# First-block slabs in halves and in place, evictions ahead of weight quarters, a reordered gate stage, and values computed inside the differential heads

## The reference

```python
# first block
mod = silu(c) @ w_ada + b_ada                      # c (1, 1024), w_ada (1024, 6144)
sh1, sc1, g1, sh2, sc2, g2 = split(mod, 6)
mix = token_mixer(x * (1 + sc1) + sh1)             # 8 attention heads of 64 over 64 keys chosen
                                                   # by an indexer, and a gated convolution,
                                                   # group norms, @ w_out
x = layer_norm(ALPHA * x + g1 * mix, ln1_g, ln1_b)
ff = (silu(h @ w_gate) * (h @ w_up)) @ w_down      # h = x * (1 + sc2) + sh2
x = layer_norm(ALPHA * x + g2 * ff, ln2_g, ln2_b)
# second block, i = 0 with gla_mixer, i = 1 with diff_attn_mixer
h = h + mixer(rms_norm(h, norm_mix[i]))
h = h + swiglu_2(rms_norm(h, norm_ffn[i]), ffn_w_in[i], ffn_w_out[i])
h = h + sigmoid(rms_norm(h, ple_norm[i]) @ ple_w_gate[i]) * (p[i] @ ple_w_proj[i])
# gla_mixer: q, k, v, r, zf, zb = h @ w_in; gates log_sigmoid(z @ w_gate + b) / 16;
#   chunked linear attention both ways, 4 heads; out = (rms_norm(o) * silu(r)) @ w_out
# diff_attn_mixer, 8 heads: q, k = rope(rms_norm(.)), a = softmax(q1 k1) - lam * softmax(q2 k2),
#   out = rms_norm(a @ v, g_sub) * (1 - lambda_init) @ w_out
```

## Time and profile before

| what | us |
|---|---|
| runs | 1121.69, 1120.24, 1120.56 |
| median | 1120.56 |
| the profiled execution | 1117.48 |
| its span | 1115.6 |
| PE busy | 1056.9 (95%) |
| DVE busy | 722.0 (65%) |
| ACT busy | 554.9 (50%) |
| POOL busy | 224.9 (20%) |
| mean granted TensorE clock | 0.987 of full |

### The profile page before, as it was taken

How to read it: one execution, slowest core, us unless ns; L and a number is a source line. 1 busy time by engine, 2 the same in 40 slices (tenths; PEclk the granted TensorE clock), 3 DMA queues, 4 the chain that set the end, 5 groups by cost and what they waited for, 6 DMA issues and landing times.

```text
span 1115.6 us, 20267 instructions
## 1 busy us (share of the span) xinstructions
PE 1056.9 (95%) x7901; PEld 980.8 (88%) x7901; DVE 722.0 (65%) x1127; ACT 554.9 (50%) x956; POOL 224.9 (20%) x248
## 2 busy tenths in 40 slices
PE   5999988999999899999999999989996999999998
PEld 5577677999999697889999999978874999999998
DVE  4785777776754657768565655666769765655654
ACT  2223555554453675527454544655447764544453
POOL 0110002233311021012333310141210223332102
PEclk9999989999999999999999999989999999999999
DMA  9972464567566353504555456644430265544651
GB/s 351 401 274 76 151 228 150 170 226 265 160 174 192 124 179 139 212 1 147 193 188 181 149 157 189 230 145 158 147 139 18 76 227 180 196 143 143 204 190 39
DMA packets 183556, 192.78 MB, mean 173 GB/s; under 512 B 5881, under 2 KB 143394, under 8 KB 183490
## 3 DMA queue, kind: packets, MB, share of 16 engines
q1 hardware_dynamic: 182480, 191.15, 50.8%
q0 software_dynamic: 144, 0.52, 0.2%
q10 hardware_dynamic: 866, 0.21, 0.1%
HBM read 190.83 MB, written 1.05 MB: 172 GB/s over the span
## 4 chain that ended last, share of the span: by engine, by line
PE 54%; DVE 5%; ACT 3%; issue 2%; POOL 1%; POOLq 0%; ACTq 0%
PE gemm L2047 17%; PE gemm L2049 17%; PE gemm L2048 16%; DVE wlo L1361 1%; PE aux L2522 1%; ACT whi L874 1%; DVE neg_max L2000 1%; PE aux L2578 1%; PE aux L2572 1%; DVE d_p L2016 1%; DVE state L1913 0%; DVE g_b L1867 0%; ACT ohi L1110 0%; ACT om L1112 0%; ACT d_p L1316 0%
## 5 line engine op out<-in xcount | busy, mean ns | idle before, releaser
L1361 DVE TENSOR_TENSOR wlo<-raw,whi 128x1024 fp32r<-128x1024 f32 (+2 forms) x324 | 369.2, 1184 | 77.9 <-ACT whi L874 77.4
L2047 PE MATMUL gemm<-ohi,whi 128*128 128x256 f32 x1376 | 388.8, 283 | 1.5 <-DVE wlo L1361 1.3
L2048 PE MATMUL gemm<-olo,whi 128*128 128x256 f32 x1376 | 385.8, 280 | 0.0
L2049 PE MATMUL gemm<-ohi,wlo 128*128 128x256 f32 x1376 | 384.3, 279 | 0.0
L874 ACT ACTIVATE whi<-raw 128x1024 fp32r<-128x1024 f32 (+2 forms) x324 | 288.7, 956 | 65.7 <-PE gemm L2049 51.0
L2047 PEld LDWEIGHTS gemm<-ohi,whi 128*128 128x128 f32 x1376 | 259.7, 189 | 4.9 <-issue 2.5
L2048 PEld LDWEIGHTS gemm<-olo,whi 128*128 128x128 f32 x1376 | 259.9, 189 | 0.6 <-issue 0.5
L2049 PEld LDWEIGHTS gemm<-ohi,wlo 128*128 128x128 f32 x1376 | 259.8, 189 | 0.0
L2049 PE MATMUL gemm<-acthi,wlo 128*128 128x256 f32 x528 | 147.8, 280 | 0.0
L2047 PE MATMUL gemm<-acthi,whi 128*128 128x256 f32 x528 | 147.5, 279 | 0.0
L2048 PE MATMUL gemm<-actlo,whi 128*128 128x256 f32 x528 | 147.3, 279 | 0.0
(11 more groups left out here) (364 smaller groups left out, 1515.7 us busy)
## 6 DMA issues: line engine op xcount, KB each, us to landing
raw<-in_ffn_w_in SPq DMA_DIRECT2D x44, 1024.0 KB, 6.1
raw<-in_ffn_w_out SPq DMA_DIRECT2D x32, 704.0 KB, 5.7
part<-in_w_ada SPq DMA_DIRECT2D x32, 512.0 KB, 10.6
raw<-in_gla_w_in SPq DMA_DIRECT2D x6, 2048.0 KB, 7.7
raw<-in_diff_w_in SPq DMA_DIRECT2D x6, 2048.0 KB, 7.7
raw<-in_w_gate SPq DMA_DIRECT2D x11, 1024.0 KB, 6.3
raw<-in_w_up SPq DMA_DIRECT2D x11, 1024.0 KB, 8.5
raw<-in_w_down SPq DMA_DIRECT2D x16, 704.0 KB, 5.4
```

The costliest lines, as they stand in the source:

```text
L1361: dve.tensor_tensor(wlo[hslot][:, q * w:(q + 1) * w], raw[slot][:, q * w:(q + 1) * w], whi[hslot][:, q * w:(q + 1) * w].bitcast(F32), ALU. ...
L2047: pe.matmul(dst, st_hi, mv_hi, start=start, stop=False)
L2048: pe.matmul(dst, st_hi, mv_lo, start=False, stop=False)
L2049: return pe.matmul(dst, st_lo, mv_hi, start=False, stop=stop_)
```

## The change

Out of the ring: ada0 and ada1 are loaded in halves as ada2 and ada3 are; TensorE's share of them is now two k tiles of slab 0 and one of slab 1, and it sums slab 1 before it transposes x. The two slabs of w_out are loaded into the places of `wlo[0]` and `wlo[1]` (`out_w`), where VectorE's low part overwrites them; the first is loaded when in_q's tiles are done, the second when 18 parts are used. Ten part buffers are filled at first instead of eight. Parts 8, 9 and 10 are multiplied before the heads, the modulation sums 5 to 8 come at heads 0, 1, 3 and 5. ScalarE splits out0's first slab during in_gc, VectorE makes its low parts before the first head, and the second slab's quarters are made in heads 5 and 6 and behind the last norm. The first out0 block goes in pairs of k tiles, with the last head's values and group sums between; out0 evicts first. In the layer norms ScalarE squares the mean from PSUM, and VectorE makes the first `om`. gla_q becomes WIDE and comes before gla_z; the squares are summed by VectorE. The second half of silu and the table load move behind the first `kd_tok`. In ple_gate1 and ple_gate2 quarters move behind evictions, ScalarE's operand of tile m-1 comes behind sigmoid m, the last two products are VectorE's. diff_v is made in 64 steps of 256 columns: 16 before the heads, six within each.

```diff
+DIRECT = {0: 2, 1: 1}
-    ada = lambda i: Phase(f"ada{i}", 1, SLAB, 0, 1, by="mod", ahead=False, ring=i < 2, slot=i % 2)
+    ada = lambda i: Phase(f"ada{i}", 1, SLAB, 0, 1, by="mod", ahead=False, ring=False, slot=i % 2)
-        Phase("out0", 2, SLAB, 4, 1, slot=1), *ffn(0),
+        Phase("out0", 2, SLAB, 4, 1, ring=False, slot=1), *ffn(0),
+        out_w = [sb(f"out_w{i}", SLAB, at=place[f"wlo{i}"]) for i in range(2)]
-            return (n % 8, n // 8) if n < 16 else (8 + n % 2, (n - 16) // 2)
+            return (n % 10, n // 10) if n < 18 else (8 + n % 2, 1 + (n - 18) // 2)
-        WIDE = ("gate_up0", "out1", "out2")
-        EVICT_FIRST = ("out1", "out2", "ple_gate1", "ple_gate2")
-        DONE_BEFORE = {"gate_up0": 4, "gate_up1": 2, "gate_up2": 2, "diff_q": 2}
+        WIDE = ("gate_up0", "gla_q", "out1", "out2")
+        EVICT_FIRST = ("out0", "out1", "out2", "ple_gate1", "ple_gate2")
+        DONE_BEFORE = {"out0": 4, "gate_up0": 4, "gate_up1": 2, "gate_up2": 2, "diff_q": 2}
...
+            if at.i == 0 and ph.name in ("ple_gate1", "ple_gate2"):
+                return {0: (1, 2, 3)}.get(t, ()) if act else {0: (0, 1), 1: (2, 3)}.get(t, ())
...
+            def load_out(i):
+                sp.wait_ge(*((tile_done, PH["in_q"].tile0 + 4), (part_used, 18))[i])
+                sp.dma_start(flat(out_w[i], KT, 512), kmaj(a["w_out"][0], 0, 512, i)).then_inc(out_in[i], 16)
-                      ("in_hc", 0): parts(*range(8, 18)),
-                      ("out0", 0): parts(*range(18, 24)), ("gate_up0", 0): parts(24, 25),
+                      ("in_hc", 0): [*parts(10, 11, 12, 13), lambda: load_out(0), *parts(14, 15, 16, 17)],
+                      ("in_gb", 0): [*parts(18, 19), lambda: load_out(1), *parts(*range(20, 24))],
+                      ("gate_up0", 0): parts(24, 25),
...
-            PARTS_OF_HEAD = ((8, 9), (10, 11), (12, 13), (14, 15), (16, 17), (18, 19), (20,), (21,))
+            PARTS_OF_HEAD = ((11, 12), (13, 14), (15, 16), (17, 18), (19, 20), (21,), (22,), (23,))
+            for q in range(4):
+                low(PH["out0"], At(0), q)
+            modulate_part(10)
...
             pe.wait_ge(lo_ready, 4 * (PH["out0"].j0 + 1))
-            out_columns(0, range(4), OUT_ORDER[0:4], True, False)
+            out_columns(0, range(4), OUT_ORDER[0:2], True, False)
+            values(NH - 1)
+            group_stats((3,), C("blk"), mix_sq, X[0:1])
+            out_columns(0, range(4), OUT_ORDER[2:4], False, False)
+            group_stats((1,), C("blk"), mix_sq, X[1:2])
+            out_columns(0, range(4), OUT_ORDER[4:6], False, False)
             banks.claim(X[3], mod_read)
             modulation(9)
-            out_columns(0, range(4), OUT_ORDER[4:8], False, True)
+            out_columns(0, range(4), OUT_ORDER[6:8], False, True)
...
+            gemm("gla_q", dve_read, olo_from=start)
             ph = PH["gla_z"]
             for k in range(KT):
-                pe.wait_ge(olo_ready, start + k + 1)
...
-            gemm("gla_q", dve_read, after=lambda at, t: stats(tok=True) if t == 2 else None)
-            keep_warm(X[2], 2)
+            stats(tok=True, summed=gla_summed)
...
                     me.did(act.activation(kd_tok[:, :], G[1][:, :], ACT.Copy), kt_ready)
                 if h == 0:
+                    silu_half(1)
+                    log_exp()
...
                     act.wait_ge(ple_in, n + 1)
                     act.activation(tl(sg, t % 2), tl(gt, t % 2), ACT.Sigmoid).then_inc(ple_sig, 1)
+                    if k == 1 and 0 < m < KT - 1:
+                        operand(m - 1)
...
-            gemm("diff_v", v_ready, shape="token", operand=(dhi, xlo), after=lambda at, t: partners(6 + t) if at.i == 0 else None)
-            pe.wait_ge(qk_ready, 8)
-            pe.wait_ge(v_ready, 8)
+            value_steps(0, 8)
+            partners(6)
+            partners(7)
+            value_steps(8, 16)
...
             for i in range(NH + 2):
                 if i + 1 < NH:
                     scores(i + 1)
+                if i >= 2:
+                    h = i - 2
+                    banks.claim(X[2], mixed_ready)
+                    me.next(pt_ready)
+                    if h % 2 == 0:
+                        pe.wait_ge(v_ready, 4 + h // 2 + 1)
...
+                if i < NH:
+                    value_steps(16 + 6 * i, 22 + 6 * i)
+                if i in (6, 8):
+                    group_stats((i // 2 - 3,), ones[:, :], d_nsq, X[1:2])
                 if 1 <= i <= NH:
...
# VectorE, per head step
+                if i >= 3:
+                    me.next(pv_done)
+                    me.did(dve.tensor_copy(tl(d_o, i - 3), X[2][:, 0:T]), mixed_ready)
+                if i in (0, 1):
+                    low(*VALUES, 2 + i)
+                if 3 <= i <= 6:
+                    low(*OUT2, i - 3)
# ScalarE, per head step
+                if i in (2, 5, 7):
+                    take_values({2: 1, 5: 2, 7: 3}[i])
+                if 3 <= i <= 6:
+                    ahead(*OUT2, i - 3)
```

More of the change, by code:

```diff
@@ L539, in build @@
         sources = {
-            **{f"ada{i}": columns(ada, 512 * ADA_ORDER[i]) for i in range(2)},
             "in_gc": columns(w_in, C_GC), "in_hc": columns(w_in, C_HC), "in_gb": columns(w_in, C_GB),
-            "out0": columns(a["w_out"][0], 0),
             "gate_up0": gate_up(a["w_gate"][0], 0, a["w_up"][0], 0), "down0": down(a["w_down"][0]),
@@ L573, in quarters @@
                 each = (4, 0, 0, 0)
+            elif first and ph.name in ("ple_gate1", "ple_gate2"):
+                each = (1, 0, 0, 0) if act else (0, 0, 0, 0)
             elif ph.name in EVICT_FIRST:
@@ L641, in _ @@
                 if not ph.ring:
+                    for more in behind.get((ph.name, 0), ()):
+                        more()
                     continue
+                if ph.name in ("in_gc", "in_hc"):
+                    sp.wait_ge(mod_done, 1 + ph.slot)
                 def load(at, ph=ph):
@@ L984, in gemm @@
                 rounds(act, ph, body)
-            def split_all(name, free=None, qs=range(4)):
-                if free:
-                    wait(act, tile_done, PH[free].tile0 + 4)
-                for q in qs:
-                    split(PH[name], At(0), q)
             def take(name, t, dst, ready):
@@ L1025, in _ @@
                 take("in_gc", t, tl(gc, t), gc_ready)
+                for q in {0: (0, 1), 2: (2, 3)}.get(t, ()):
+                    split(PH["out0"], At(0), q)
             act.wait_ge(lam_sum, 1)
@@ L1099, in layer_norm @@
                     ahead(PH["gate_up0"], At(0), 0)
[L1100 to L1101 removed]
+                me.next(mean_done)
+                me.seen(mean_done)
+                me.did(act.activation(sq_sum[:, :], X[0][:, 0:T], ACT.Square, scale=1.0 / D), mean_squared)
                 me.next(var_ready)
@@ L1185, in next_quarters @@
                     ahead(PH[name], At(0), q)
-            gemm("gla_q")
+            for q in range(3):
+                ahead(PH["gla_q"], At(0), q)
             root(X[0], T + 2, 1.0 / D, 1, rstd[:, :])
+            ahead(PH["gla_q"], At(0), 3)
             gemm("gla_k")
@@ L1297, in _, with take_values @@
                 gemm(name, after=after)
-            gemm("diff_v", evac(v_dst(d_v), v_ready, v_scale))
+            VALUES, OUT2 = (PH["diff_v"], At(0)), (PH["diff_v"], At(1))
+            def take_values(j):
+                wait(act, tile_done, PH["diff_v"].tile0 + j + 1)
+                bank = VALUE_BANKS[j]
+                for tt in range(TT):
+                    ins = act.activation(d_v[:, tt * D + 256 * j:tt * D + 256 * (j + 1)], bank[:, tt * 256:(tt + 1) * 256],
+                                         ACT.Copy, scale=v_scale(tt))
+                me.did(ins, v_ready)
+            for q in range(4):
+                ahead(*VALUES, q)
+            take_values(0)
             def pair_root(g, bank):
@@ L1850, in _ @@
                 take_q(At(0), t, bank_of(PH["gla_q"], At(0), t)[0])
+            low(PH["gla_k"], At(0), 3)
             for b in range(4):
@@ L1982, in _ @@
                 gemm(name, scaled(d_q if base == 0 else d_k, qk_src), after)
-            gemm("diff_v", None, lambda at, t: turn(6 + t) if at.i == 0 else None)
+            VALUES, OUT2 = (PH["diff_v"], At(1)), (PH["out2"], At(0))
+            low(*VALUES, 0)
+            low(*VALUES, 1)
+            turn(6)
+            turn(7)
             make_tile = group_make(d_o, d_nsq, lambda t: lam[:, 5:6])
```

247 lines of the change are left out of this document (142 added, 105 removed).

## The result

The changed kernel takes 1128.63 us (median of four runs, 1128.54 to 1131.93) against 1120.70 us (four runs) of the kernel before: ratio 1.0082, 95% interval 1.005 to 1.0113. It is slower by 0.8%, where the forecast was 1092.9 us and faster. The profiled execution took 1128.56 us, span 1126.8 us against 1115.6.

What follows compares the result with a forecast made beforehand. TensorE's gaps and low-clock time, not its matmul work, were taken as the gain available. Terms 9.9 + 3.5 + 1.5 + 3.5 + 9.3 = 27.7 us gave 1092.9 us from a median of 1120.56; range 1083 to 1106.

Steps and rivals of the forecast that it cites:

- Differential heads: diff_v and heads: values between head steps, mean 4.43 us per head, gain 9.3 us, bounds 4 and 12.
- third rival: Differential heads close into one chain, 12.5 us a head if nothing overlaps, kernel 1149 us, slower; chance 0.05.
- break-even of 8.4 us: Differential heads: mean period per head above which the kernel becomes slower than before, (59.5 + 18.4 - 7.5 - 11.7)/7.
- Front: First block up to the first scores: halves of ada0 and ada1 gain 0.85 us, bounds 0 and 1.65.
- it doesn't last: First block: the 1.65 us earlier first om is lost, since part 4 lands at 47.65 whatever comes before.
- Sparse heads: First block's heads: moved modulation and earlier root against a late part 20, gain 0.15 us, bounds -3 and 3.
- wait for part 20: First block's heads: part 20 lands some 4 us after VectorE wants it, making TensorE wait about 2 us.
- out0 and its sums: End of first block: out0 ends 6.2 us earlier (bounds 3, 7.5), its sums gain 2.8 us (bounds 1.5, 3.5).
- two adds of 0.74: out0's sums: GpSimd's adds left after evicting first, beside tile 6's eviction of 0.47 and square of 0.42 us.
- Norm, gates, silu: First norm -0.1 us; second norm and gates 3.5 us, bounds 1.5 and 4.5; silu behind kd_tok 1.5 us.
- ple_gate1: ple_gate1 up to diff_q: TensorE's wait moves from weights to operand, gain 3.5 us, bounds 1 and 5.4.
- a gain of 2.8: ple_gate1: gain if the exclusive lock lets two low parts hold GpSimd's product, 0.7 us more for tile 5.

Runs made afterwards that it cites:

- e1: The changed kernel with diff_v and the eight differential heads put back as before; 1113.50 us, ratio 0.9942 to the kernel before.
- e2: The changed kernel with ScalarE's high part of out2's quarter ahead of the wait for the transposes in head steps 3 to 6; 1110.65 us, ratio 0.9911.
- e3: The changed kernel with VectorE's low part of out2's quarter made one head step later (steps 4 to 7); 1109.35 us, ratio 0.9888.
- e4: The changed kernel with VectorE's copy of d_o ahead of the maxima of the same step; 1122.22 us, ratio 1.0014.
- e6: On e3, VectorE's last two low parts in ple_gate1 and ple_gate2 stand behind tiles 5 and 6, one each; 1104.49 us, ratio 0.9846.
- e7: On e3, the two ple stages put back as before; 1107.69 us, ratio 0.9879.
- e8: On e3, four idle warming matmuls ahead of the gates' products; 1106.77 us, ratio 0.9869.
- e9: On e3, slab 1 with two k tiles on TensorE again and its sums behind the transposes of x; 1109.00 us, ratio 0.9882.
- e5: On e3, VectorE multiplies parts 4 and 5 behind the rotations of keys and index queries; 1105.84 us, ratio 0.9872.

## Why the prediction was wrong, point by point
**Differential heads: the step that failed.** The prediction added up each engine's work in a head and walked the first steps through. Those were right: the first scores (811.05, or 815.5 on the clock of before, forecast 815.1), and 3.8 to 4.7 us a step for the first ones, forecast 4.43. It then used that rhythm for all eight heads and priced the quarters of out2 in steps 3 to 6 as 1.2 us of VectorE's and 1.04 us of ScalarE's time. Where they stand in the queues it didn't follow. "A head then costs TensorE 4.6 us ... 5.05 us with one" counts loads, and a ring is a sum of latencies over engines: from 834.90 on, product 1.4, six steps of values 3.3 (partly at the low clock), transposes 0.6, copy 0.5, high part 1.1, low part 1.1, maxima and scaling 1.4, copy 0.5 are the 9.9 us. The third rival was near it. It had the bank, the copy and the maxima, and the length (12.5 us, measured 9.9), but it doesn't name the quarter that closes the ring (its term of 1.2 us may be the low part; none fits the high part of 1.1), and it was given 0.05 because the same hand-overs ran at 3.5 us a head before; before, no quarter of another stage stood among them. Its break-even of 8.4 us also took the other gains as 18.4 us: with the 4.4 us that came it is (59.5 + 4.4 - 7.5 - 11.7)/7 = 6.4 us, and the mean from the first to the last product with d_v was (876.02 - 821.84)/7 = 7.7. With the ring open the values in the heads are worth 2.8 to 5.8 us (102.9 to 99.9 us for the stretch against 105.7), forecast 9.3: the tail still waits for ScalarE's last eviction of values and runs three engines deep.

**Front, -0.85 forecast, +2.7 measured.** The landing of part 4 was right (47.56), and so was that VectorE has more to do ahead of the first scores. The sum took the durations from rows in which VectorE ran alone, and it didn't ask what the earlier keys do to GpSimd: 2.2 us for two parts, then a wait of 2.12 us, and behind it a clock of 0.66 of full from 55 to 65. The steps "SyncE's queue is otherwise in the same order" and "it doesn't last" stood on DMA times alone. That an earlier engine meets something new was not in the sum.

**Sparse heads, 0.15 forecast, 2.1 lost** (+2.7 to +4.8). 1.7 us of it lie in head 0, where the products of in_hc run at the low clock (16 of them in 5.4 instead of 3.7 us). The cause is open: TensorE's wait ahead of them is 0.76 to 0.77 us in after, e1 to e4 and e6 to e9 alike (0.73 in before), and they take 3.7 us in e1, e2 and e7 and 5.4 in the others, with the same code. The wait for part 20 came as walked through: VectorE stands 3.78 us for it at 130.35 (forecast some 4), and TensorE 1.66 us at 132.80 (forecast 2).

**out0 and its sums.** From the transposes of the last head to the end of out0 the gain was 5.9 us (+4.8 to -1.1), forecast 6.2; the gap and the low clock of the earlier trace rows went as said. The sums' wait fell from 3.44 to 2.41 us, forecast 2.8 us of gain with both shifts together and measured 1.0: a low part still stands between the last two evictions (175.72 in after) and the folding ahead of them (172.21). The term that was mis-sized is "two adds of 0.74": beside the low part one of them takes 1.63 us (175.88).

**Norm, gates, silu.** The norm gave 0.3 (forecast -0.1). Up to the gates' products the gate stage gave 3.6 us and to gla_k's first product 3.0 (forecast 3.5); thirty products later 2.0 are left in after, e1 and e5, and 0.3 to 0.4 in e2 to e4, e6, e7 and e9, because the low clock behind the bare wait stays longer on gla_k's products than in before. The forecast took the bare wait in and left the clock behind it out; a step of gla_q takes 1.41 us and is covered from the third on, the bare wait is 2.09 us (forecast 2.1). The silu gave 1.5 us as forecast; its second half and the table load (1.28 us, to 467.55) were done before the next kd_tok at 468.54.

**ple_gate1, 3.5 forecast, 0 measured.** The wait moved for the most part from the weights to the operand (1.03 us for wlo, then 0.88 and 3.50 for xlo), and the last low part came at 744.55, 1.8 us earlier on the clock of before, not 3.9. The two low parts in a row were priced at nothing since "the weights' low parts are done in tiles 4 and 5". The Trainium skill (SBUF - State Buffer, Who interferes with whom) was weighed there: it calls the shared port an exclusive lock, and the prediction made of it a gain of 2.8. The trace agrees with the lock, instruction by instruction: GpSimd's product (735.05) ends 0.6 us behind the first low part (735.65), the second low part is then held and takes 1.76 us instead of 1.21, GpSimd's next add (736.22) ends 0.6 us behind that one, and xlo (737.26) takes 0.95 instead of 0.48. So one low part holds the product, not two, and the delay goes on to everything behind; both prices were too good. The other 1.8 us went to the clock: it is 0.69 from 741 to 752 as before, but in before TensorE ran there on products whose last operand came at 750.99 anyway, and now on products that nothing else holds up.

**What the runs leave open.** A drift of 1.2 us between 187 and 311 us, in stages that the change doesn't touch (products 0.1178 us apart in after, 0.1167 in before); e2, e3 and e4 have 0.1167 there with the same code (e7 has 0.1178), so it belongs to that execution. TensorE in 20 us of it, in before and in after (174 and 172 records):

```profile
202.00:222.00 20.00, 20.00 (x174) 20.00 (x173) 13.63 (x18) 9.29 (x16) 4.88 (x6) 1.00 0.60 203
```

```profile
200.00:220.00 20.00, 20.00 (x172) 20.00 (x172) 13.54 (x18) 9.25 (x16) 4.90 (x6) 1.00 0.60 202
```

Why the same wait is followed by the low clock in one execution and not in another, as in head 0, behind the gates and in the last heads, was not found. The 0.2% that the prediction gives as what can be told is too good: the intervals above reach 0.2 to 0.4% to either side.

## What to carry to other kernels
When work of another stage is slipped into a pipelined loop, write down for each slipped instruction what it waits for and what is queued behind it on its engine, and follow the chain until it ends or returns: a ring costs the sum of its latencies in every round, whatever the engines' loads. An instruction whose input another engine makes in the same step belongs one step later; that one move was worth 1.7% here. And when a step comes earlier, look at what it now runs beside, on another engine or in a queue, before counting the gain.

## What the runs showed of the hardware
VectorE and GpSimd hold each other up by whole instructions: a product of VectorE that is issued while GpSimd multiplies ends 0.3 to 0.6 us behind GpSimd's (2.31 instead of 0.75 us at 48.65 in after; a product with a scalar 2.22 instead of 0.48 in e7), and the other way round (1.20, 1.63 and 1.71 instead of 0.74 us for GpSimd's at 735.05, 175.88 and 736.22 in after). The Trainium skill (SBUF - State Buffer, Who interferes with whom) says that a VectorE instruction with two inputs in SBUF contends with GpSimd's reads; the trace agrees (2.31 against 0.75 us). A wait of 2.12 us at 56.5 was followed by a clock of 0.66 of full from 55 to 65 (the level of 1.2 GHz for part of the time): from the start of the index heads' first products (56.51) to the wait for relu that ends at 66.96 it is 10.5 us, and 7.5 in before (56.79 to 64.28), 3.0 us of TensorE's time on top of the wait. But the same wait is followed by different clocks: 0.83 over those 10 us in e4 (wait of 2.11 us), and behind 0.77 us in head 0 the same products take 3.7 us in three kernels and 5.4 in six. And the distance of full-clock products comes in two sizes, 0.1167 and 0.1178 us, that change along one execution and, from 197 to 311 us, between executions of the same code.
